# Sliding-window mixer of a hybrid encoder layer: attention scores of two tiles issued together in every second block

## The reference, cut to what matters

```python
xn = rms_norm(h, norm_mix); proj = xn @ w_in          # qA kA vA | qB kB vB
sc = einsum('bcqhgd,bckhd->bchgqk', qc, kb) * HEAD_DIM ** -0.5
sc = where(valid, sc + bias, NEG_INF)
probs = softmax(concatenate([sc, sink], -1), -1)[..., :-1]
oa = einsum('bchgqk,bckhd->bcqhgd', probs, vb)
ob = differential_attention(qb, kb, vb, ...)
h = h + concat(oa, ob) @ w_out
h = h + gated_conv_ffn(rms_norm(h));  h = h + sigmoid(rms_norm(h) @ Wg) * (p @ Wp)
out = rms_norm(h)
```

## Time and profile before

| what | value |
|---|---|
| median of three executions | 1230.97 us (1227.92 to 1232.18) |
| span of the profiled execution | 1229.7 us (the page gives no other time for it; 1.3 us below the median) |
| TensorE busy | 1197.1 us, 97% of the span |
| VectorE, ScalarE, GpSimd busy | 867.3, 517.8, 250.2 us |
| mean granted TensorE clock | 0.992 of full speed |
| stage A, 118 to 206 us | TensorE busy 87.14 of 88.00 us, VectorE 66.84, ScalarE 53.08 |

### The profile page before, as it was taken

How to read it: one execution, slowest core, us unless ns; L and a number is a source line. 1 busy time by engine, 2 the same in 40 slices (tenths; PEclk the granted TensorE clock), 3 DMA queues, 4 the chain that set the end, 5 groups by cost and what they waited for, 6 DMA issues and landing times.

```text
span 1229.7 us, 17128 instructions
## 1 busy us (share of the span) xinstructions
PE 1197.1 (97%) x6167; PEld 1001.8 (81%) x6167; DVE 867.3 (71%) x1514; ACT 517.8 (42%) x1045; POOL 250.2 (20%) x291
## 2 busy tenths in 40 slices
PE   8999999999888999999999999999999999999997
PEld 7998887788676888888888888888888888888886
DVE  5433786877886577877787777877777999964443
ACT  4312665565655224433343343343344444733321
POOL 0000000344455122232332323323210000000000
PEclk9999999999899999999999999999999999999999
DMA  7464233111831512242322333233499533620101
GB/s 217 89 90 91 50 89 76 42 40 69 222 139 42 164 52 81 82 128 94 121 87 89 125 103 112 95 94 112 146 345 312 172 95 103 225 75 26 43 35 51
DMA packets 127916, 136.08 MB, mean 111 GB/s; under 512 B 15714, under 2 KB 93274, under 8 KB 127770
## 3 DMA queue, kind: packets, MB, share of 16 engines
q1 hardware_dynamic: 127834, 135.00, 36.1%
HBM read 96.77 MB, written 37.22 MB: 109 GB/s over the span
## 4 chain that ended last, share of the span: by engine, by line
PE 61%; issue 4%; DVE 2%; POOL 1%; ACT 1%; POOLq 0%; DVEq 0%; ACTq 0%
PE ps L1723 60%; PE ps L1729 1%; DVE xs L1474 1%; DVE h L1469 0%; DVE conv L1410 0%; POOL stat L687 0%; ACT xs L796 0%; DVE act_t L1185 0%; POOL stat L706 0%; POOL bias_a L712 0%; POOL more_f L714 0%; PE ps L2118 0%; ACT wbuf L793 0%; POOL o_t L709 0%; DVE h L1688 0%
## 5 line engine op out<-in xcount | busy, mean ns | idle before, releaser
L1723 PE MATMUL ps<-act_t,wbuf 128*128 128x512 f32 x1200 | 280.1, 389 | 0.5 <-DVE a_buf L1499 0.5
L1723 PEld LDWEIGHTS ps<-act_t,wbuf 128*128 128x128 f32 x1200 | 225.2, 188 | 47.5 <-DVE a_buf L1499 0.8
L1723 PE MATMUL ps<-wbuf 128*128 128x512 f32 x912 | 214.8, 390 | 0.0
L1723 PEld LDWEIGHTS ps<-wbuf 128*128 128x128 f32 x912 | 170.6, 188 | 35.1
L1723 PE MATMUL ps<-act_t,wq 128*128 128x512 f32 x624 | 152.2, 396 | 3.6 <-DVE wq L1187 3.0
L1723 PEld LDWEIGHTS ps<-act_t,wq 128*128 128x128 f32 x624 | 114.3, 188 | 30.8 <-issue 7.5
L687 POOL TENSOR_TENSOR stat<-stat 128x1 f32<-128x1 f32 x32 | 17.6, 549 | 420.9 <-DVE stat L1194 420.9
L793 ACT ACTIVATE wbuf<-raw 128x512 fp32r<-128x512 f32 (+1 forms) x107 | 69.0, 646 | 73.9 <-PE ps L1723 63.8
L1723 PE MATMUL ps<-hx,wbuf 128*128 128x512 f32 x408 | 95.7, 389 | 0.0
L1185 DVE TENSOR_TENSOR wbuf<-raw,wbuf 128x512 fp32r<-128x512 f32 (+1 forms) x107 | 87.4, 818 | 11.5 <-ACT wbuf L793 11.2
L1723 PEld LDWEIGHTS ps<-hx,wbuf 128*128 128x128 f32 x408 | 76.5, 188 | 15.9
(11 more groups left out here) (208 smaller groups left out, 1962.8 us busy)
## 6 DMA issues: line engine op xcount, KB each, us to landing
u_ops<-wbuf_f SPq DMA_DIRECT2D x77, 256.0 KB, 2.2
raw<-u_ops SPq DMA_DIRECT2D x77, 256.0 KB, 2.7
raw<-in_w_ffn_in SPq DMA_DIRECT2D x33, 512.0 KB, 3.8
g_ffn<-in_w_ffn_in SPq DMA_DIRECT2D x11, 512.0 KB, 3.9
act_f<-in_w_ffn_out SPq DMA_DIRECT2D x21, 256.0 KB, 4.3
w_raw<-in_w_in SPq DMA_DIRECT2D x10, 512.0 KB, 4.4
wbuf_f<-in_w_ffn_out SPq DMA_DIRECT2D x18, 256.0 KB, 5.9
x_in<-in_x SPq DMA_DIRECT2D x8, 512.0 KB, 3.8
```

Source lines behind the costliest of these rows:

```text
L1723: return nc.tensor.matmul(dst, lhs, rhs, start=start, stop=stop)
```

## The change

TensorE: the order inside a block becomes transposes of tile n-2, value products of tile n-3, then, in even blocks alone, the scores of tiles n and n+1, then the half unit. The wait ahead of the scores becomes one for the logits of both tiles before (`S.a_logits` at n, it was n-1). VectorE: the block's work is split into `a_logit(n)` and `a_rest(n)`; odd blocks keep the order logits, rest; even blocks have rest, logits. So the logits of tile n (even) and of tile n+1 stand next to each other. ScalarE, GpSimd and SyncE keep their programs.

```diff
+        def a_rest(n):
             if n >= 3:
 ...
+        for n in range(NA + 3):
+            if n < NA and n % 2 == 1:
+                a_logit(n)
+            a_rest(n)
+            if n < NA and n % 2 == 0:
+                a_logit(n)
             fill_lo(a_fill(n))
@@ TensorE
         for n in range(NA + 3):
-            if n < NA:
-                s, t = n // NT, n % NT
-                if n >= 2:
-                    pe.wait_ge(S.a_logits, n - 1)
...
+            if 2 <= n <= NA + 1:
+                m = n - 2
+                pe.wait_ge(S.a_probs, m + 1)
+                if m >= 1:
+                    pe.wait_ge(S.a_tlo, m)
+                for j in range(4):
+                    ins = nc.tensor.transpose(ps[:, 5, P * j:P * (j + 1)], e_a(m)[:, P * j:P * (j + 1)],
+                                              ident[:, :])
+                ins.then_inc(S.a_turned, 1)
             if n >= 3:
                 m = n - 3
                 pe.wait_ge(S.a_tlo, m + 1)
...
                 ins.then_inc(S.a_pv, 1)
-            if 2 <= n <= NA + 1:
...
+            if n < NA and n % 2 == 0:
+                if n >= 2:
+                    pe.wait_ge(S.a_logits, n)
+                a_score(n)
+                a_score(n + 1)
             if NA <= n < NA + 2:
                 b_score(n - NA)
             if a_fill(n) is not None:
                 unit(FIRST_UNITS + a_fill(n) // 2, a_fill(n) % 2)
```

More of the change, by code:

```diff
@@ L1332, in fill_lo @@
                 after_unit(FIRST_UNITS + part // 2)
-        for n in range(NA + 3):
-            if n < NA:
[L1336 to L1356, removed]
@@ new lines, in a_logit @@
+        def a_logit(n):
+            s = n // NT
+            o = 32 * (n % 2)
+            dve.wait_ge(S.a_scores, n + 1)
+            if n >= 3:
+                dve.wait_ge(S.a_turned, n - 2)
+            for j in range(4):
+                g, c = j // 2, j % 2
+                k0 = first_key(n, c)
+                ins = nc.vector.tensor_tensor_reduce(
+                    out=e_a(n)[:, P * j + k0:P * (j + 1)],
+                    in0=ps[:, 1 + 2 * (n % 2) + g, P * c + k0:P * (c + 1)],
+                    in1=bias_a[:, s, g, k0:P], scale=1.0, scalar=LOWEST, op0=ALU.add, op1=ALU.max,
+                    accum_out=small[:, o + j:o + j + 1])
+                if k0:
+                    nc.vector.memset(e_a(n)[:, P * j:P * j + k0], 0.0)
+            link(ins)
+            sink = [sinkt[:, 4 * x + 2 * s:4 * x + 2 * s + 2].unsqueeze(2).to_broadcast([P, 2, 2]) for x in range(2)]
+            mx, neg, dif = (small[:, o + 4 * x:o + 4 * x + 4].rearrange("p (g c) -> p g c", g=2) for x in range(3))
+            link(nc.vector.scalar_tensor_tensor(out=neg, in0=mx, scalar=-1.0, in1=sink[1], op0=ALU.mult,
+                                                op1=ALU.min))
+            nc.vector.tensor_tensor(dif, neg, sink[0], ALU.add).then_inc(S.a_logits, 1)
@@ L1842, in b_score, with a_score @@
                             ins.then_inc(S.b_scores, 1)
-        for n in range(NA + 3):
-            if n < NA:
-                s, t = n // NT, n % NT
-                if n >= 2:
-                    pe.wait_ge(S.a_logits, n - 1)
[L1849 to L1860, removed]
+        def a_score(n):
+            s, t = n // NT, n % NT
+            if t == 0 and s == 1:
+                pe.wait_ge(S.unit_lo, 10)
+            for c in range(2):
+                ch = 2 * t + c
+                k0 = first_key(n, c)
+                for m, (a, b) in enumerate(SPLIT3):
+                    for g in range(2):
+                        rows = slice(HD * g, HD * g + HD)
+                        ins = mm(ps[:, 1 + 2 * (n % 2) + g, P * c + k0:P * (c + 1)],
+                                 q_a[rows, s, a, ch, :, :].rearrange("p u q -> p (u q)"),
+                                 k_a[rows, b, (ch - 1) * CHUNK + k0:(ch + 1) * CHUNK], m == 0, m == 2)
+            ins.then_inc(S.a_scores, 1)
+        for n in range(NA + 3):
+            if 2 <= n <= NA + 1:
[3 more added lines that the diff above has]
+                    pe.wait_ge(S.a_tlo, m)
+                for j in range(4):
+                    ins = nc.tensor.transpose(ps[:, 5, P * j:P * (j + 1)], e_a(m)[:, P * j:P * (j + 1)],
+                                              ident[:, :])
+                ins.then_inc(S.a_turned, 1)
             if n >= 3:
```

## The result

| | median us | executions |
|---|---|---|
| before | 1229.29 | 11, 1227.69 to 1232.18 |
| after | 1232.59 | 11, 1231.55 to 1234.88 |

The ratio after to before is 1.0025, with a 95% interval of 1.0016 to 1.0034: 2.0 to 4.2 us slower. The forecast was 5.0 us slower. Its 1236.0 us also stood on the three executions known then, whose median (1230.97) lies 1.7 us above that of all eleven.

What follows compares the result with a forecast made beforehand. A closed ring through ScalarE and VectorE was to bind stage A: start to 138.35, six rounds with splits and a long store 63.4, end 9.1, so 210.9 against 205.91: 5.0 us slower, 1236.0 us; range 1229.5 to 1239.5 with rivals.

Steps and rivals of the forecast that it cites:

- the delay is passed on whole: Behind stage A: stage B and what follows are full, so the whole 5.0 us reaches the kernel's time.
- the ring: Closed path in stage A from even tile's transposes through ScalarE and VectorE to the next: 10.31 us per pair against TensorE's 9.76.
- The long store: ScalarE's output copy waits for the previous tile's store; four stores ahead of weight loads can be long, 0.6 us taken.
- The start: Stage A from the first tiles' logits, at 123.30, to the transposes of tile 2, put at 138.35.
- The end: Last two blocks of stage A, with stage B's first scores: 9.1 us, last value products starting at 210.9.
- The splits: VectorE's low parts of unit and weights in every second odd block: 0.31 us more per such pair, 10.62; three counted.
- The handing over: TensorE's passage from unit to scores, up to 0.17 us, avoided by the new order: -2.7 to 0 us over 16 blocks.
- the first rival: Ring under 9.76 us, TensorE stays the bound, only handing over counts: -2.7 to 0, say -1.4 us, 1229.6 us; chance 0.14.
- the ring that doesn't bind: The first rival: stage A's transposes never wait and TensorE stays the bound, 1229.6 us; chance 0.14.
- gift back in stage B: Rival: part of the 5 us vanishes in TensorE's 17.3 us idle in stage B; 3 us gives 1233; chance 0.11.
- the clock: Part of the dearer rival (chance 0.10): idle stretches drop TensorE's clock to 1.2 GHz; one fall gives 1238.5 us.
- the stores: Part of the dearer rival (chance 0.10): all four stores long gives 1237.8 us, with a clock fall 1240.3.

Runs made afterwards that it cites:

- e6: Changed kernel with VectorE's low part of the weights moved into the next even block, behind the even tile's logits: stage A 88.21 us, ratio to before 1.0017.
- e11: Changed kernel with VectorE's probabilities ahead of the low parts and the weights' low part behind the even tile's logits: stage A 84.59 us, ratio to before 0.9987.
- e3: Changed kernel with value products ahead of transposes, paired scores behind both, and VectorE's old order (logits first in every block): stage A 84.50 us, ratio to before 0.9983.
- e5: e3 with the pair of scores moved to the head of even blocks: stage A 84.34 us, ratio to before 0.9990.
- e1: Changed kernel with VectorE's reordering taken back (logits first in every block), TensorE's new order kept: stage A 90.44 us, ratio to before 1.0038.

## Why the prediction was right in kind and wrong in size

The mechanism was right: idle brackets at even tiles' transposes alone, ended by the probabilities (line 1374), though three of the eight are under the forecast's 0.4 us; odd tiles free; rounds of two lengths, but for the two around tile 8 (9.99 and 10.70); clock at 1.00 in stage A; stage B unchanged. That the delay is passed on whole fits the times, whose interval of 2.0 to 4.2 us would still allow 1.5 us given back. The size was not right: 3.50 us in stage A instead of 5.0. And the chance of 0.66 stood on slower by over 0.3%, where 0.25% (0.16 to 0.34) was measured.

The step that failed is the sum. It put a round of the ring at 10.31 us, 0.55 over TensorE's 9.76, and the round measured 10.20; it counted 0.6 us for a late store that never held anything up; and its start was too long. Four terms differ.

- **The ring, 10.31 forecast, 10.20 measured.** Two of its hops were taken too long. From the start of the probabilities to the transposes it is 0.75 (155.41 to 156.16), not 0.69 + 0.14 = 0.83: I took the 0.14 from a projection unit that VectorE releases, and transposes start sooner behind their release. From transposes to value products it is 0.42, where I chose 0.45 between 0.38 and 0.55. The other eight agree within 0.02 us each (the low parts at 148.00 apart, which the split held up in this round). Over six rounds, whose mean without the splits is 10.20, this makes 0.7 us. A ring that exceeds TensorE's work by half a microsecond turns an error of one per cent in the ring into one of a fifth in the result.
- **The long store, 0.6 forecast, none.** I let one of four stores land late. In the changed kernel the longest landing of a low part's store is 3.1 us, inside the 3.14 that the ring allows, and no copy waited for a store.

```profile
DMA to landing us min/median/max: 2.3/2.3/3.1
```

- **The start, 18.59 us forecast** from the first scores to the transposes of tile 2 (119.76 to 138.35), 18.25 measured (117.21 to 135.46): 0.3 less.
- **The end**, 9.1 us from the transposes of tile 14 forecast, 9.30 measured (197.56 to 206.86): 0.2 more.

Together -0.7 - 0.6 - 0.3 + 0.2 = -1.4, of 1.5 us. The splits came as forecast: 10.50 instead of 10.20 us, 0.30 against 0.31, and e6, which takes them off the ring, gives 10.20 in their place, but for the round from tile 8.

The handing over had no effect, as said: whatever TensorE gains on a ring that it waits for is swallowed. Without the waits its gain is 1.6 to 1.8 us (e11, e3, e5), inside the bounds of 0 to 2.7 and near the 1.4 of the first rival, but in part by luck. In e11, with TensorE's program as changed, a half unit in front of transposes takes 2.81 to 2.93 us and not 2.74, so most pairs of blocks gain 0.14 there and not 0.34; as much comes from the paired scores, 1.48 instead of 1.62, for which the sum had no term, and the other hand-overs take 0.08 back.

The Trainium skill (TensorEngine Tiling (Array Packing), Key Properties) says that changing the tiling mode drains the engine. The prediction's estimate of 1.4 us counted one such change fewer per pair. That this is the reason for the gain isn't shown. By the tiles in the rows (unit and transposes both have 128\*128, where the prediction lets all four differ) a pair has six changes before and five in e5 and e11; but e3 has six as well and gains 1.65 us all the same.

So 3.50 us is a loss of 5.1 us by waiting (89.65 - 84.59) less a gain of 1.6.

Of the rivals, the ring that doesn't bind gave the right time for a kernel that this change is not (e11). No gift back in stage B is seen (181.49 us of work there against 181.66), and neither the clock (1.00 in stage A) nor the stores made it dearer.

One thing the forecast left out: it said that the earlier place of the odd tile's logits gains nothing, and had no term for what VectorE's new order gives. In even blocks low parts and probabilities no longer stand behind the logits, and that is worth 0.79 us under TensorE's new order (89.65 against 90.44 in e1). In e1 the odd block alone, from value products over copies and low parts to the probabilities, holds up TensorE: 4.38 us where 3.97 are needed. So the path through the even tile's logits, which the prediction walked, isn't the only one that binds when transposes stand at the head of a block.

## What to carry to other kernels

In a hand-ordered pipeline over several engines, look for the closed path through the queues, not for the busy engine: add start-to-start distances along it and compare one round with the bound engine's work for the same round. What sits directly at the head of a block on the bound engine has no cover, so put work in front of the piece with the longest dependence. And when a change has a gain and a loss in one, undo each half and dose the path with a known operation: an operation that costs its full length lies on the ring, one that costs less than half does not throughout, and the lengths round by round show where it does.

## What the runs showed of the hardware that was not expected

The first scores of stage A started between 116.8 and 117.3 us in eight profiles and between 119.4 and 120.6 in the other five, whatever the kernel. The windows of TensorE from 20 to 30 us tell them apart (columns: stretch, length, busy, granted clock, DMA share, GB/s); first the kernel before, then the changed one:

```profile
20.00:30.00 10.00, 8.12 (x49) 0.83 0.45 148
```

```profile
20.00:30.00 10.00, 9.24 (x66) 1.00 0.60 170
```

The five late ones show a mean granted clock of 0.83 to 0.88 there, so part of that stretch ran at the lower level of 1.2 GHz; the eight early ones show 1.00. In it TensorE waited 1.8 us for one tile's normalised inputs in the kernel before, and 0.7 us in the changed one. It then ran the same 48 products in 8.78 us (from 26.36) and in 7.31 us (from 25.28).

The longer wait is 1.1 us and the slower products 1.5 us: together the whole 2.55 us between the two starts of stage A. That is most of the effect measured here, and it differs from one execution to the next: hence stage lengths, not spans.
